# Attention of a hybrid decoder step: index pages from two engines, scores among q chunks, q left unnormalised, V as the moving operand

## The reference

```python
q = rms_norm(q.reshape(b, t, N_HEADS, HEAD_DIM), g_q)
k = rms_norm(k.reshape(b, t, N_KV_HEADS, HEAD_DIM), g_k)
ki = rms_norm(ki, g_kidx)
s = jnp.einsum('bthd,bsd->bths', qi, ki)
score = jnp.einsum('bths,bth->bts', jax.nn.relu(s), wi) * INDEX_SCALE
_, idx = lax.top_k(score, ksel)          # 64 keys for the prompt, 256 for a sample
...                                      # gather keys and values by idx
logits = jnp.einsum('btngd,btsnd->btngs', qg, kg) * ATTN_SCALE
p = jax.nn.softmax(jnp.where(valid, logits, -jnp.inf), axis=-1)
out = jnp.einsum('btngs,btsnd->btngd', p, vg)
```

## Time and profile before

| | |
|---|---|
| median of three runs | 1705.25 us (1703.71 to 1705.34) |
| the profiled execution | 1706.35 us, span 1704.7 us |
| PE busy | 1503.2 us (88% of the span) |
| PEld busy | 1340.8 us (79%) |
| DVE busy | 1157.8 us (68%) |
| ACT busy | 840.5 us (49%) |
| POOL busy | 371.7 us (22%) |
| moved by DMA | 398.27 MB, mean 234 GB/s |
| first matmul of the output projection (L498) | 405.66 us |

### The profile page before, as it was taken

How to read it: one execution, slowest core, us unless ns; L and a number is a source line. 1 busy time by engine, 2 the same in 40 slices (tenths; PEclk the granted TensorE clock), 3 DMA queues, 4 the chain that set the end, 5 groups by cost and what they waited for, 6 DMA issues and landing times.

```text
span 1704.7 us, 27830 instructions
## 1 busy us (share of the span) xinstructions
PE 1503.2 (88%) x10637; PEld 1340.8 (79%) x10637; DVE 1157.8 (68%) x1598; ACT 840.5 (49%) x1250; POOL 371.7 (22%) x415
## 2 busy tenths in 40 slices
PE   6695387898799998698859999999999999999995
PEld 4554232668689998588849999999999999999994
DVE  5059777112465554577447888898888888888883
ACT  2111222102333333454326777777777777777772
POOL 3422100010299996000010020030202012020000
PEclk9898556666899999799969999999999999999998
DMA  8133300026245565351615999999999999999991
GB/s 352 58 99 107 107 1 0 28 72 259 111 153 212 210 254 197 142 187 44 263 52 216 356 352 381 353 371 361 373 367 357 375 349 377 358 377 353 376 359 26
DMA packets 64046, 398.27 MB, mean 234 GB/s; under 512 B 8226, under 2 KB 25698, under 8 KB 36002
## 3 DMA queue, kind: packets, MB, share of 16 engines
q1 hardware_dynamic: 52018, 362.79, 56.0%
q0 software_dynamic: 10112, 31.47, 6.1%
q10 hardware_dynamic: 1776, 2.14, 0.3%
HBM read 379.42 MB, written 16.95 MB: 233 GB/s over the span
## 4 chain that ended last, share of the span: by engine, by line
PE 78%; DVE 9%; ACT 4%; issue 4%; POOLq 1%; DMA 1%; POOL 1%; ACTq 0%; SPq 0%; DVEq 0%
PE ps L933 10%; PE ps L934 10%; PE ps L935 10%; PE ps L498 5%; PE ps L956 5%; PE ps L958 5%; PE ps L500 5%; PE ps L957 5%; PE ps L499 5%; PE ps L713 4%; DVE ring_lo L1396 1%; PE ps L583 1%; PE ps L634 1%; PE ps L686 1%; PE ps L653 1%
## 5 line engine op out<-in xcount | busy, mean ns | idle before, releaser
L934 PE MATMUL ps<-ring_lo,split 128*128 128x256 f32 x1056 | 298.8, 283 | 0.0
L933 PE MATMUL ps<-split 128*128 128x256 f32 x944 | 269.8, 286 | 1.5 <-DVE split L1827 1.5
L935 PE MATMUL ps<-split 128*128 128x256 f32 x944 | 267.8, 284 | 0.0
L1396 DVE TENSOR_TENSOR ring_lo<-ring,chunk_hi 128x1024 fp32r<-128x1024 f32 x100 | 134.8, 1350 | 157.0 <-ACT chunk_hi L1010 156.9
L1775 DVE TENSOR_TENSOR ring_lo<-ring,split 128x2048 fp32r<-128x2048 f32 x88 | 201.6, 2291 | 45.5 <-ACT split L1255 45.1
L1010 ACT CAST chunk_hi<-ring 128x1024 fp32r<-128x1024 f32 x100 | 104.9, 1049 | 223.3 <-PE ps L500 172.0
L934 PEld LDWEIGHTS ps<-ring_lo,split 128*128 128x128 f32 x1056 | 199.8, 189 | 4.8
L933 PEld LDWEIGHTS ps<-split 128*128 128x128 f32 x944 | 179.7, 190 | 5.8 <-issue 1.9
L500 PE MATMUL ps<-xn_lo,chunk_hi 128*128 128x288 f32 x608 | 184.1, 303 | 0.0
L935 PEld LDWEIGHTS ps<-split 128*128 128x128 f32 x944 | 179.8, 190 | 0.0
L1255 ACT CAST split<-ring 128x2048 fp32r<-128x2048 f32 x88 | 169.1, 1922 | 0.0
(11 more groups left out here) (305 smaller groups left out, 3498.0 us busy)
## 6 DMA issues: line engine op xcount, KB each, us to landing
ring<-wmoe SPq DMA_DIRECT2D x132, 1536.0 KB, 8.8
arena<-wmoe SPq DMA_DIRECT2D x44, 1536.0 KB, 8.9
ring<-wpre SPq DMA_DIRECT2D x41, 1536.0 KB, 6.5
s_b<-arena POOLq DMA_DIRECT2D x8, 640.0 KB, 3.3
arena<-s_b SPq DMA_DIRECT2D x8, 640.0 KB, 4.4
arena<-cki POOLq DMA_DIRECT2D x64, 64.0 KB, 2.1
arena<-ck SPq DMA_DIRECT2D x32, 128.0 KB, 3.1
arena<-cv POOLq DMA_DIRECT2D x32, 128.0 KB, 2.8
```

Of the source, the lines that this page charges most:

```text
L933: mm(o, xg_hi[:, e % 2, k, :], hi[:, c], start=(k == 0), stop=False)
L934: mm(o, xg_hi[:, e % 2, k, :], lo[:, c], start=False, stop=False)
L935: m = mm(o, xg_lo[:, e % 2, k, :], hi[:, c], start=False, stop=(k == KD - 1))
L1396: V.tensor_tensor(ring_lo[:, n % RING, w], ring[:, n % RING, w], chunk_hi[:, c % 2, :], ALU.subtract).then_inc(S["chunk_lo"], 1)
```

## The change

It has seven parts, all in the attention.

*Index pages.* POOL issues those of sequences 0 to 3, SP those of 4 to 7, between weight units 2 and 3, after a wait for the constants and the table. The index matmuls wait for both semaphores. Within a pair of sequences they now go part by part, so that neighbours alternate between the two column groups.

*Scores among q chunks.* The 16 score steps of the prompt move from behind the transposes of k to between q chunks 3 to 7 (4, 3, 3, 3 and 3 steps), with two pairs of PSUM banks instead of three. The matmuls of k and v then wait for the last of the 16 relus. On TensorE, before, from the weighted sums of the index scores (L569) on; L486 are q chunks, L583 k and v, L595 sums of squares of q, L602 transposes of k, L614 prompt score steps:

The core of the diff:

```diff
-KV_SLOTS = {1: (4, 5, 0), 2: (1, 2, 3)}
+KV_SLOTS = {1: (1, 2, 3), 2: (4, 5, 0)}
+PI_IN_Q = (4, 3, 3, 3, 3)
+ROUNDS_FIRST, ROUNDS_EACH = 8, 3
+KIDX_BY_POOL = 4
+KV_SEM = (0, 1, 1, 3)
...
-        for n in range(U_WO):
+        for n in range(3):
+            load_unit(n)
+        sp.wait_ge(S["const"], 80)
+        for b in range(KIDX_BY_POOL, NB):
+            for j in range(NPG):
+                r = page(sp, b, j)
+                sp.dma_start(kidx[:, b, j * PG:(j + 1) * PG],
+                             dr["cki"][bass.ds(r, 1)].rearrange("a p k -> p (a k)")).then_inc(S["kidx_sp"], 16)
...
+            if b == 6:
+                sp.wait_ge(S["sl_mm"], 1)
...
+        sp.wait_ge(S["so_mm"], 2)
+        for n in range(U_WO, U_WO + 3):
+            load_unit(n)
         sp.wait_ge(S["so_mm"], 3)
-        for n in range(U_WO, U_WO + 6):
+        for n in range(U_WO + 3, U_WO + 6):
             load_unit(n)
...
+        def p_index(it):
+
+            qk, c = it // 8, it % 8
+            nk = 128 * (qk + 1)
+            if it == 0:
+                pe.wait_ge(S["sc"], 1)
+            if it >= 2:
+                pe.wait_ge(S["pi_relu"], it - 1)
+            for r in range(2):
+                m = mm(ps[:, 4 + 2 * (it % 2) + r, 0:nk], qi[64 * r:64 * r + 64, c, qk * 128:(qk + 1) * 128],
+                       kit[64 * r:64 * r + 64, 0:nk], start=True, stop=True)
+            m.then_inc(S["pi_mm"], 1)
...
         for c in range(3, 8):
             q_chunk(c)
+            for _ in range(PI_IN_Q[c - 3]):
+                p_index(it)
+                it += 1
...
-                pe.wait_ge(S["sc"], 1)
+                pe.wait_ge(S["pi_relu"], 16)
...
+        pe.wait_ge(S["q_sq"], 1)
+        for qk in range(2):
+            for c in range(8):
+                mm(ps[:, 7, 16 * qk + 2 * c:16 * qk + 2 * c + 2], sqq[:, c * T + qk * 128:c * T + qk * 128 + 128],
+                   pairsum[:, 0:128:64], start=True, stop=True)
+        pe.wait_ge(S["q_sqb"], 1)
+        for bp in range(4):
+            for b2 in range(2):
+                for p in range(2):
+                    o = slice(64 * b2 + 32 * p, 64 * b2 + 32 * p + 32)
+                    m = mm(ps[o, 7, 32 + bp:33 + bp], sqb[:, 2 * bp + b2, p].rearrange("q r g t -> q (r g t)"), ones[:, 0:1],
+                           start=True, stop=True)
+        m.then_inc(S["q_ss"], 1)
...
+                for b2 in range(2):
+                    b = 2 * bp + b2
+                    for p in range(2):
+                        o = slice(64 * b2 + 32 * p, 64 * b2 + 32 * p + 32)
+                        rhs = past_keys(b)[:, p, c0:c0 + nn] if i < 2 else kt[:, p, TP:T]
+                        m = mm(ps[o, base + i, 0:nn], qb[:, b, p].rearrange("q r g t -> q (r g t)"), rhs, start=False, stop=True,
+                               skip_group_check=True)
...
+            bank = 3 * (bp % 2)
+            for j in range(9):
+                nk = 128 if j < 8 else NS
+                for b2 in range(2):
+                    o = slice(64 * b2, 64 * b2 + 64)
+                    w = past_values(2 * bp + b2, j) if j < 8 else vn[0:NS, 2, :]
+                    m = mm(ps[o, bank, 0:256], pt[0:nk, j, o], w, start=(j == 0), stop=(j == 8))
             m.then_inc(S["so_mm"], 1)
+            pe.wait_ge(S["so_c"], bp + 1)
+            for p in range(2):
+                m = nc.tensor.transpose(ps[:, bank + 1, p * 128:(p + 1) * 128], out_s[:, p * 128:(p + 1) * 128], ident)
+            m.then_inc(S["so_t"], 1)
...
+        act.wait_ge(S["q_ev"], 8)
+        act.wait_ge(S["pi_acc"], 16)
+        a(sqq, q.rearrange("p a b -> p (a b)"), ACT.Square).then_inc(S["q_sq"], 1)
...
+        act.wait_ge(S["q_ss"], 1)
+        a(rq[:, 0:36], ps[:, 7, 0:36], ACT.Sqrt, bias=eps, scale=1.0 / HD).then_inc(S["q_rt"], 1)
...
+        a(kt[:, :, 0:TP], ps[:, 0:2, 0:TP], ACT.Copy, scale=param("gq")).then_inc(S["kt"], 1)
...
+                      bias=stt[:, 4 + g:5 + g], scale=rq_p[:, qk, 4 * (n // 2) + g, n % 2:n % 2 + 1],
...
+        def s_out(bp):
+            act.wait_ge(S["so_mm"], bp + 1)
+            act.wait_ge(S["sl_n"], bp + 1)
+            if bp:
+                act.wait_ge(S["so_t"], bp)
+            a(out_s, ps[:, 3 * (bp % 2), 0:256], ACT.Copy, scale=v(B_RS, 4)[:, bp:bp + 1]).then_inc(S["so_c"], 1)
...
-        topk(sc[0:NS, :], st[0:NS, 112:120], 16)
...
-            qh = q[:, 4 * hf:4 * hf + 4, :].rearrange("p a b -> p (a b)")
-            V.scalar_tensor_tensor(out=qh, in0=qh, scalar=param("gq"), in1=rq, op0=ALU.mult, op1=ALU.mult
-                                   ).then_inc(S["q_st"], 1)
...
+        for qk in range(2):
+            nk = 128 * (qk + 1)
+            acc = scp[:, qk, 0:nk]
             topk(acc, st[:, 112:120], TOPK_P // 8)
             V.scalar_tensor_tensor(out=selp[:, qk, 0:nk], in0=acc, scalar=-2.0e38, in1=nc01[:, qk, 0:nk],
                                    op0=ALU.is_gt, op1=ALU.max).then_inc(S["selp"], 1)
+        topk(sc[0:NS, :], st[0:NS, 112:120], ROUNDS_FIRST)
...
+        dve.wait_ge(S["q_rt"], 1)
+        link(V.reciprocal(rq[:, 0:36], rq[:, 0:36]))
+        V.tensor_scalar(rq[:, 0:36], rq[:, 0:36], ATT_SCALE, None, ALU.mult).then_inc(S["rq"], 1)
...
+                m = V.tensor_scalar(qb[o, :, p, r], src, param("gq")[o], None, ALU.mult)
...
+            V.tensor_tensor(stt[:, 4:8], stt[:, 0:4], own, ALU.mult).then_inc(S["pl_mx"], 1)
...
-            V.tensor_scalar(prob[bp % 2], prob[bp % 2], stt[:, 3:4], None, ALU.mult).then_inc(S["sl_n"], 1)
+            V.reciprocal(v(B_RS, 4)[:, bp:bp + 1], stt[:, 2:3]).then_inc(S["sl_n"], 1)
...
+            dve.wait_ge(S["so_t"], bp + 1)
...
-        for b in range(NB):
+        for b in range(KIDX_BY_POOL):
...
+            pool.wait_ge(S["q_sq"], 1)
+            qs = sqq.rearrange("p (a b) -> p a b", a=KD)
+            for r in range(2):
+                o = slice(64 * r, 64 * r + 64)
+                for p in range(2):
+                    m = g.tensor_copy(sqb[o, :, p, r], qs[o, 4 * p:4 * p + 4, TP:T].rearrange("p g (b t) -> p b g t", b=NB))
+            m.then_inc(S["q_sqb"], 1)
```

More of the change, by code:

```diff
@@ L107 @@
 B_SELP = B_SCP + 512
-B_END = B_SELP + 256
+B_RQ = B_SELP + 256
+B_RS = B_RQ + 48
+B_OS = B_RS + 48
+B_END = B_OS + 256
 D_H = A_PH
@@ L557, in _ @@
                 pe.wait_ge(S["relu"], bp - 1)
[L558 to L564 removed]
+            for part in range(3):
+                for b2 in range(2):
+                    b = 2 * bp + b2
+                    w = qib[:, b].rearrange("p r c t -> p (r c t)")
+                    o = slice(64 * b2, 64 * b2 + 64)
+                    if part < 2:
+                        m = mm(ps[o, base + part, :], w, kidx[:, b, part * 512:(part + 1) * 512], start=True, stop=True)
+                    else:
+                        m = mm(ps[o, base + 2, 0:NS], w, kit[:, TP:T], start=True, stop=True)
             m.then_inc(S["idx"], 1)
@@ L1064, in _ @@
             cp(q[:, c, :], ps[:, c % 4, 0:T]).then_inc(S["q_ev"], 1)
+            for _ in range(PI_IN_Q[c - 3]):
+                p_relu(it)
+                it += 1
+        act.wait_ge(S["q_ev"], 8)
+        act.wait_ge(S["pi_acc"], 16)
+        a(sqq, q.rearrange("p a b -> p (a b)"), ACT.Square).then_inc(S["q_sq"], 1)
         for i, (t0, nt) in enumerate(BLK):
@@ L1574, in p_max @@
             link(V.tensor_reduce(stt[:, 0:4], src, AX.X, ALU.max, negate=True))
-            V.tensor_scalar(stt[:, 4:8], stt[:, 0:4], ATT_SCALE, None, ALU.mult).then_inc(S["pl_mx"], 1)
+            n, qk = groups[i]
+            own = rq_p[:, qk, 4 * (n // 2):4 * (n // 2) + 4, n % 2]
+            V.tensor_tensor(stt[:, 4:8], stt[:, 0:4], own, ALU.mult).then_inc(S["pl_mx"], 1)
         def p_norm(i):
```

189 lines of the change are left out of this document (71 added, 118 removed).

## The result

The changed kernel takes 1621.4 us (median of four runs, 1620.28 to 1625.35) against 1705.3 before: 0.9501 of the time, with an interval from 0.9486 to 0.9515. The forecast was 1629, with a range of its own from 1619 to 1639. The profiled execution has a span of 1618.5 us against 1704.7. The first matmul of the output projection, L521 now, starts at 322.05 instead of 405.66, so 83.6 of the 86.2 us lie ahead of it, and 2.6 behind.

What follows compares the result with a forecast made beforehand. Attention ahead of the output projection was taken as the bound: index -17.2, scores among chunks +9.4, VectorE's order and reciprocals -40, loop +14, sample stage -41, so 76 us less and 1629. Own range 1619 to 1639; 8 in 10, 1606 to 1652.

Steps and rivals of the forecast that it cites:

- Index pages: Early attention: with POOL and SP sharing the issue, index matmuls wait only for the mask, starting at 72.0 instead of 85.07.
- Score steps and VectorE's order: Attention before the first logits: score steps among q chunks add 9.4 us; the new VectorE order brings first logits at 163.
- The sign of 1 us gaps behind each chunk: Sign of being right: TensorE has gaps of about 1 us behind each q chunk, where prompt scores now stand.
- VectorE's order and the lost reciprocals: VectorE's path to the first logits: the new order and the removed reciprocals over q's norms together give -40 us.
- Prompt loop: First maximum to sample scores: three selection rounds per step instead of two make it 100 us instead of 86.2.
- not in two values: Sign of being right: maxima in the prompt loop stand 11 and 13 us apart.
- Sample values: Value stages: 18 matmuls with 64-column weights take 5.5 us each, between 4.2 at full clock and 8.4 at half.
- its worst case: Value stages at half clock without overlap take 15.3 us each, for a total time of 1668 us.
- I keep this pitch, 0.445 each: 4.4 a stage: Sample scores: neighbours overlap only in pairs as before, so 4.4 us a stage with the mask, 6.4 for the first.
- the rival of four tiles abreast: Sample scores: four column groups work at once, stages lose 1.6, 1.9, 1.5 and 1.9 us; total 1623 us; chance 0.18.
- its V pages come some 10 us early: Sample stage: the last pair's value pages, issued behind the first value stage, land some 10 us before they are needed.
- a scaled copy and two transposes on the path, 1.1: Sample value stages: each gains a scaled copy and two transposes on the path, 1.1 us.

Runs made afterwards that it cites:

- the last experiment: The changed kernel measured again unchanged, on the chip of two other follow-ups, and profiled a second time: 1618.72 us (0.9488).
- The experiment with 16 rounds: The changed kernel with 16 selection rounds ahead of the prompt loop and 2 per step, instead of 8 and 3: 1630.32 us (0.9549).
- the grouped order: The changed kernel with sample scores group by group again, three parts of one column group and then the next: 1624.06 us (0.9514).
- the mended sample stage: The changed kernel with ScalarE copying transposed probabilities before the next exponential, and weight units 7 to 9 issued after the last value pages: 1615.66 us (0.9463).

## Why the prediction was right

Boundary by boundary, with the second profile of the changed kernel beside the first:

| | forecast | first | second |
|---|---|---|---|
| index matmuls start | 72.0 | 75.97 | 72.56 |
| k and v start | 117.4 | 122.03 | 118.62 |
| first logits | 163 | 167.61 | 164.21 |
| sample scores start | 267 | 268.57 | 264.98 |
| output projection starts | 330 | 322.05 | 316.28 |

*Index pages.* POOL was done at 47.7 and SP at 45.6, at 1.09 us per index page instead of the 1.35 of a key page, which is twice the size. (On POOL size makes no difference: index pages and value pages go out 1.14 us apart.) Weight unit 3 held nothing up. The first profile starts its index matmuls 4 us late, the second 0.6; what differs between the two stands in the last experiment.

*Score steps and VectorE's order.* Five chunks and 16 steps took 30.2 us, forecast 29.6 (29.4 by its own terms). The sign of 1 us gaps behind each chunk did not show: the waits there are 0.26, and 0.70 ahead of k and v. From the last accumulation to the second mask 14.3 (14.3), the eight rounds 21.0 (21.0), norm to first logits 8.2 (8). The reciprocals were on the path, which the run without them shows (16.3 of 17.5). The prediction put VectorE's order and the lost reciprocals in one term, and that term holds. Within it the place of the scores, which brings the accumulations forward, is worth nothing by itself, as the run with the scores behind k and v shows.

*Prompt loop.* From the first maximum to the sample scores 97.0 us, forecast 100 between 93 and 105. Maxima stand 9.5 to 13.3 apart and not in two values, so that sign was wrong. The experiment with 16 rounds bears out the mechanism: more than half of a third round is hidden.

*Sample values.* 5.82, 4.3, 5.8 and 5.87, together 21.8, forecast 22.0. The form was decisive, as the run with V as weights shows. That the sum agrees to 0.2 is luck: 5.5 was a choice between 4.2 at full clock and 8.4 at half, no row had it, and the granted clock was 0.72 or 0.73 in three stages and 1.00 in one. (The 15.3 of its worst case is not what its rows give either: twice 8.4 is 16.8.)

*Where it was off: the sample scores.* The step "I keep this pitch, 0.445 each: 4.4 a stage" failed. The stages took 2.5 us each, 10 instead of 19.6, the price of the rival of four tiles abreast, which had 0.18. Its time, 1623, is nearer than the forecast. I had taken from the earlier trace rows that a matmul overlaps only with its neighbour, when that row could not show more: in its order most neighbours are in the same group. The second, smaller miss is "its V pages come some 10 us early": they came 1.84 us late, because the sample stage was faster and because the pages, issued beside weight units 7 to 9, took a median of 7.1 us to land there. The last key pages, "needed at 302", were waited for too, 1.17 us, since the scores ahead of them were done at 293.9. The third is "a scaled copy and two transposes on the path, 1.1" at each stage: between two value stages they cost nothing (2.75 us with them, 2.72 without). Scores -9.6, waits for pages +3.0 and these -2.5 make up most of the sample stage's 53.5 instead of 63 us.

*What was luck.* Errors of both signs met. The first logits came 4.6 us late, the loop was 3 shorter, the sample stage 9.5 shorter. Without the late start the run would lie under the forecast's own range, as it does by a hair in the second set of runs (1618.72). The pitch of the scores, which failed, decides little: with the old order the sample stage is 3.1 us longer and not 9.6, and the run's 2.7 us are not clear of noise.

*What stays open.* Why the granted clock falls in the first, third and fourth value stage of the first profile, and not in the grouped order or in the mended sample stage, no run here separates; in the second profile the fourth ran at 1.00. The swap of slots, the earlier issue of weight units 7 to 9 and the part-by-part order of the index matmuls were not run alone.

## What to carry to other kernels

An overlap that a trace shows is bounded by the order in which it was taken: before it is used as a pitch, ask whether neighbours could have run abreast there at all. When a change frees one engine on a path, list what the other engine does in its waits: here four selection rounds in such waits, and the norm of k ahead of the last ones, brought the first maximum 12.7 us forward. A stage that becomes shorter starts to wait for its last transfers, so their issue is part of its price.

## What was not expected of the hardware

TensorE runs the same 24 fp32 passes of 32-column tiles in 2.00 us or 4.60 us at the same clock, by their order alone. The same value stage takes 4.25 us or 5.8, at a granted clock of 1.00 or 0.72, and with V as weights 16.5 at 0.50. Reciprocals over 1152 columns take 7.35 us, five times a multiplication of that size (1.42).
